# Top-k attention in four head pairs between the chunks of the output projection, with its weight pieces and both top-k searches in another order

## The chip, the cores and the metric

The kernel runs on one core of a Trainium2 chip. The metric is the device time in microseconds (us) of one execution; lower is better. The engines are TensorE (PE, matmuls; PEld, its weight loads), VectorE (DVE), ScalarE (ACT), GpSimd (POOL) and SyncE (SP, which here only issues weight transfers).

## What is computed

Four layers on 256 tokens of width 1024, in float32. The change touches one of them, the "even" layer: sparse attention and a pooling branch, whose results go through one output projection.

```python
def even_mixer(h, w_in, w_out, q_g, k_g, pool_w, pool_scale):
    q, k, v, qi, ki, wi, u = jnp.split(h @ w_in, offsets, axis=-1)
    q, k = rms_norm(q (8 heads of 64), q_g), rms_norm(k (2 heads of 64), k_g)
    attn = dsa_attention(q, k, v, qi, ki, wi)
    pooled = multiscale_pool(u, pool_w, pool_scale)     # 4 groups of 128 channels
    return concatenate([attn, pooled]) @ w_out          # 1024 x 1024

def dsa_attention(...):      # per block of 128 queries
    score = sum over 4 index heads of relu(qi . ki) * wi, causal
    sel = top_k(score, 64)                              # 64 keys of each query
    logits = q . k[sel] / 8;  p = softmax(logits);  o = p @ v[sel]
```

The kernel doesn't gather: it turns the top 64 of each query into an additive mask (0 or a very large negative number) and runs a dense softmax over all keys.

## The kernel before, in words

All weights stream through three raw buffers in SBUF (`raw_weights`), in the order that `weight_pieces()` writes out by hand; SP issues the transfer of piece n once the last use of piece n-3 is done. Each piece is cut into "halves". For every half ACT writes the rounded part (`w_hi`, line 1271) and DVE the rest (`w_lo`, line 1592) into one of four places, so half s can be written once TensorE has read half s-4. A product with a half is then three fp32r matmuls: hi*hi, hi*lo and lo*hi. The DVE and ACT programs call `advance(upto)` at fixed points, which writes all halves up to that number; a call placed behind other work waits for it, and TensorE with it.

`features` (lines 646, 647, 650) makes 128 output features of 256 tokens from a half. `out_half` (709, 710, 714) adds one chunk of 128 input channels to the output y, in 12 matmuls of 512 columns; `out_last_two` (733 to 735) does the last two chunks bank by bank, so that the four banks of y come one after the other. `add_y` (1648) adds y to x, `norm` (773, 1313, 1618) makes the normalized input of the next layer, and the feed-forward layer begins with `fresh_features` (629).

In the even layer before the change the halves are, counted from the layer's first: h0 to h3 index queries and small columns, h4 to h6 k and v (h6 is v, lines 1070 to 1072), h7 to h10 q, h11 to h14 u, then the pool's weights and h15 to h22 for the eight chunks of the output projection. TensorE, in order: projections of the index part; first half of k; the index products (1057); rest of k and v; q and u, with the sums of squares for the norms (`head_square_sums`, 907) between them; then `softmax_heads` over eight heads, one at a time: logits (1089), transposes of the probabilities (943), values (1099 to 1101); then the pool products (1116); then the eight chunks of the output projection, attention's four first.

DVE forms the score (1930 to 1936) and calls `choose` twice: eight rounds of `max` (1944) and `match_replace` (1946), with two calls of `advance` inside, and then ten small operations that form the mask (1949 to 1959). The first call, for the 256 keys of the second query block, stands behind the score. Then the three `normed` (1822) of k and q, and only then the second call, for the first block. ACT's part is the squares (1417), the inverse roots (`scale_unit`, 1424 and 1425), the exponentials (1458) and the copies of the transposed probabilities (1467). POOL makes the pool's running sums as soon as u is there (547 to 552), and splits the attention's outputs into hi and lo (`split_output`, 508 and 511). A projected block goes through the `units` 0 to 3 of PSUM in turn; unit n waits until unit n-4 has been read.

Of the kernel before, what the change touches and what calls it, by code (L numbers as in the profile page):

```python
# [49 lines left out]
def weight_pieces():  # L50
# [36 lines left out]
def units():  # L87
    out = []

    def add(stage, engines):  # L90
        out.extend((stage, e) for e in engines)

    add("norm0", "vvvv")
    add("a_f", "a" * 8)
    add("a_i", "a" * 8)
    add("a_q", "v" * 8)
    add("a_g", "a" * 8)
    add("norm1", "aaaa")
# [6 lines left out]
    add("ev_i", "aa")  # L105
    add("ev_k", "v")
    add("ev_v", "a")
    add("ev_q", "vv")
    add("ev_u", "aa")
    add("ev_pool", "vv")  # L110
# [12 lines left out]


def build(nc, a, const, mask, out):
# [7 lines left out]
    with ExitStack() as ctx:  # L133
# [83 lines left out]
        def y_bank(j, t, n):  # L217

            return ps[:, (0 if j in (1, 4) else 4) + 2 * t + n, :]
# [126 lines left out]
        for name in ("sig_ready ln_ready scan_ready exp_ready spread_ready spread_exp kin_ready "  # L346
# [6 lines left out]
                     "ev_mixed "  # L353
# [96 lines left out]
        OUT2 = 8  # L450

# [124 lines left out]
        def _(pe):  # L576
# [353 lines left out]
            def softmax_heads(pre, heads, logits, pv):  # L930

                for i in range(heads + 3):
                    if i < heads:
                        if i >= 2:
                            pe.wait_ge(st(pre + "_max"), i - 1)
                        logits(i, ps[:, 4 + i % 2, :]).then_inc(st(pre + "_logits"), 1)
                    if 2 <= i < heads + 2:
                        h = i - 2
                        pe.wait_ge(st(pre + "_prob"), h + 1)
                        if h >= 2:  # L940
                            pe.wait_ge(st(pre + "_tcopied"), h - 1)
                        for b in range(3):
                            ins = pe.transpose(ps[:, 6 + h % 2, b * P:(b + 1) * P], prob[:, h % 3, b * P:(b + 1) * P], ident)
                        ins.then_inc(st(pre + "_turned"), 1)
                    if i >= 3:
                        h = i - 3
                        pe.wait_ge(st(pre + "_tcopied"), h + 1)
                        pv(h)

# [100 lines left out]
            bank = open_unit("ev_k")  # L1050
            s = next_half("ev_kv")
            used(s, features(bank[:, 0:T], s, SELF))
            wait_read(pe, "ev_i", 1)
            for h in range(HIDX):
# [4 lines left out]
                ins.then_inc(st("ev_rel"), 1)  # L1059
            s = next_half("ev_kv")  # L1060
# [14 lines left out]
            pe.wait_ge(st("ev_relu"), HIDX)  # L1075
            head_square_sums(ones64, 16)
            project_features("ev_q", "ev_q", SELF)
            project_features("ev_q", "ev_q", SELF)
            head_square_sums(ones64, 17)
            project_features("ev_u", "ev_u", SELF)  # L1080
            head_square_sums(ones64, 18)
            project_features("ev_u", "ev_u", SELF)

            def ds_logits(h, bank):
                if h == 0:
                    wait_read(pe, "ev_q", 1)
                rows = slice(HD2 * (h % 2), HD2 * (h % 2) + HD2)
                for t in range(NT):
                    ins = pe.matmul(bank[:, P * t:P * t + P * (t + 1)], evq[rows, h // 2, t * P:(t + 1) * P],
                                    evk[rows, h // 4, 0:P * (t + 1)], start=True, stop=True)  # L1090
                return ins

            def ds_pv(h):
                if h % 2 == 0 and h >= 4:
                    pe.wait_ge(st("ds_out"), h // 2 - 1)
                rows = slice(HD2 * (h % 2), HD2 * (h % 2) + HD2)
                bank = ps[rows, (h // 2) % 2, :]
                vh = lambda s: evv[:, s, HD2 * (h // 4):HD2 * (h // 4) + HD2]
                pe.matmul(bank[:, 0:P], vh(0), probT[:, h % 2, 0:P], start=True, stop=True)
                pe.matmul(bank[:, P:T], vh(0), probT[:, h % 2, P:2 * P], start=True, stop=False)  # L1100
                pe.matmul(bank[:, P:T], vh(1), probT[:, h % 2, 2 * P:3 * P], start=False, stop=True)\
                    .then_inc(st("ds_o"), 1)

            pe.wait_ge(unit_free["a"], before("a", unit[0] - 1))
            pe.wait_ge(unit_free["v"], before("v", unit[0] - 1))
            softmax_heads("ds", HE, ds_logits, ds_pv)
            pe.wait_ge(st("ds_out"), HE // 2)
# [11 lines left out]
            out_project("ev_out", 8, OUT2, lambda k: pe.wait_ge(st("ds_split"), k + 1) if k < 4 else  # L1119
                        wait_read(pe, "ev_pool", (k - 4) // 2))  # L1120
# [134 lines left out]
        def _(act):  # L1255
# [146 lines left out]
            for u in range(4):  # L1402
# [6 lines left out]
                ("ev_k", 0), ("ev_q", 0), ("ev_q", 1)]  # L1409
# [40 lines left out]
            def softmax_heads(pre, heads):  # L1450
                for i in range(heads + 2):
                    if i < heads:
                        act.wait_ge(st(pre + "_max"), i + 1)
                        if i >= 3:
                            act.wait_ge(st(pre + "_turned"), i - 2)
                        for t, q in enumerate((Q0, Q1)):
                            c = 2 * (i % 2) + t
                            ins = act.activation(prob[:, i % 3, q], lg[:, i % 2, q], ACT.Exp,
                                                 bias=row_neg[:, c:c + 1], accum_out=row_sum[:, c:c + 1])
                            if t == 1:  # L1460
                                ins.then_inc(st(pre + "_exp"), 1)
                    if i >= 2:
                        h = i - 2
                        act.wait_ge(st(pre + "_turned"), h + 1)
                        if h >= 2:
                            act.wait_ge(st(pre + "_o"), h - 1)
                        act.activation(probT[:, h % 2, :], ps[:, 6 + h % 2, 0:S3], ACT.Copy)\
                            .then_inc(st(pre + "_tcopied"), 1)

# [39 lines left out]
            square_unit("ev_k", 0)  # L1509
            bank = unit_of("ev_v", 0)  # L1510
            act.activation(evv, bank[:, 0:T].rearrange("p (t d) -> p t d", t=2), ACT.Copy).then_inc(unit_free["a"], 1)
            scale_unit(16, HD2)
            square_unit("ev_q", 0)
            square_unit("ev_q", 1)
            scale_unit(17, HD2)
            for u in range(2):
# [3 lines left out]
                if u == 0:  # L1520
                    scale_unit(18, HD2)
            advance(unit_half[FIRST["ev_u"] + 1] + NSPLIT)
            softmax_heads("ds", HE)
# [50 lines left out]
        def _(dve):  # L1574
# [363 lines left out]
            def choose(q, n, ahead):  # L1938

                src = score[:, q]  # L1940
                for r in range(TOPK // 8):
                    if r % 4 == 2:
                        advance(ahead + r // 4)
# [4 lines left out]
                least = top8[:, 7:8]  # L1948
                dve.tensor_scalar(sel_eq[:, 0:n], score[:, q], least, None, ALU.is_equal)
# [11 lines left out]
            choose(Q1, T, e)  # L1961
            normed("ev_k", 0, 16, evk, ev_gain[:, 1:2])
            normed("ev_q", 0, 17, evq[:, 0:2, :], ev_q_gain)
            normed("ev_q", 1, 18, evq[:, 2:4, :], ev_q_gain)
            choose(Q0, P, unit_half[FIRST["ev_q"] + 1] + NSPLIT)

            def ds_out(h):
                if h % 2 == 1:
                    dve.wait_ge(st("ds_o"), h + 1)
                    if h >= 4:  # L1970
                        dve.wait_ge(st("ds_split"), h // 2 - 1)
                    dve.tensor_copy(o_full[:, (h // 2) % 2, :], ps[:, (h // 2) % 2, 0:T]).then_inc(st("ds_out"), 1)

            advance(unit_half[FIRST["ev_u"] + 1] + NSPLIT)
            softmax_heads("ds", HE, ev_bias_t, ds_out)
            for pair in range(2):
                bank = unit_of("ev_pool", pair)
                for j in range(2):
                    g = 2 * pair + j
                    link(dve.tensor_scalar(pooled[:, g, :], bank[:, j * T:(j + 1) * T],  # L1980
                                           col["ev_pool_scale_2"][:, g:g + 1], None, ALU.mult))
# [104 lines left out]
```

## Time and profile before

| | us |
|---|---|
| median of 3 runs | 1337.49 (1335.97 to 1373.87) |
| profiled execution, its own time | 1334.04 |
| its span, first to last instruction | 1332.3 |
| PE busy in the span | 1245.0 (93%) |
| DVE busy / ACT busy | 785.6 (59%) / 613.4 (46%) |
| mean granted clock of TensorE | 0.977 |

The span is what the trace's times refer to; 1.7 us lie around it. All places below are us from the span's start. The layer that the change touches lies between about 674 and 805. The granted clock is given as a share of full speed: 1.0 is 2.4 GHz, 0.5 is 1.2 GHz.

### The profile page before, as it was taken

To read this page: it belongs to the slowest core of one execution; us is meant where nothing else is said; L and a number is where in the kernel's file an instruction comes from. 1 tells how busy PE (TensorE), PEld (TensorE's weight loads), DVE (VectorE), ACT (ScalarE), POOL (GpSimd) and SP (SyncE) were. 2 spreads that over 40 slices of the span, in tenths; PEclk is the share of its full clock that TensorE was granted. 3 is DMA by queue.
4 is the path that set the end of the run, shared out by engine and by line. 5 is a ranking of instruction groups with operands and counts; after the bars stand their busy time and mean duration, and the time that the engine had idled before them with its cause. 6 is when DMAs were issued, how large, how long until landed. Compare 5 with 4: busy or idle time off the path is not lost.

```text
span 1332.3 us, 21042 instructions
## 1 busy us (share of the span) xinstructions
PE 1245.0 (93%) x8609; PEld 1139.1 (85%) x8609; DVE 785.6 (59%) x1245; ACT 613.4 (46%) x950; POOL 107.6 (8%) x172
## 2 busy tenths in 40 slices
PE   2899999998989899999998699999999999899998
PEld 2889989876789899887888479999989887899997
DVE  7888987654595354555546756555554433655554
ACT  2557623433455354554444335434453654544442
POOL 0200000031030000112100410000000133000000
PEclk9999999999999999999989589999999999999999
DMA  9896779402557465322522054555545322555552
GB/s 328 293 307 190 253 249 313 165 1 85 184 175 215 124 213 165 124 91 69 170 92 72 32 177 141 190 189 189 190 158 171 114 96 76 176 173 183 186 189 95
DMA packets 164880, 219.94 MB, mean 165 GB/s; under 512 B 5868, under 2 KB 135696, under 8 KB 164784
## 3 DMA queue, kind: packets, MB, share of 16 engines
q1 hardware_dynamic: 163984, 216.82, 50.3%
q0 software_dynamic: 800, 1.77, 0.4%
q8 instruction: 69, 1.13, 0.4%
q14 instruction: 27, 0.22, 0.0%
HBM read 217.53 MB, written 1.05 MB: 164 GB/s over the span
## 4 chain that ended last, share of the span: by engine, by line
PE 74%; DVE 12%; DMA 6%; ACT 6%; issue 2%; SPq 0%; ACTq 0%; DVEq 0%
PE ps L646 12%; PE ps L650 11%; PE ps L647 11%; PE ps L709 5%; PE ps L714 5%; PE ps L710 5%; DMA raw_weights<-in_a_w_in 4%; DVE w_lo L1592 4%; PE ps L687 3%; PE ps L682 3%; PE ps L683 3%; DVE acc L1674 2%; ACT w_hi L1271 1%; PE ps L962 1%; PE ps L907 1%
## 5 line engine op out<-in xcount | busy, mean ns | idle before, releaser
L1592 DVE TENSOR_TENSOR w_lo<-raw_weights,w_hi 128x1024 fp32r<-128x1024 f32 x348 | 423.7, 1228 | 282.3 <-ACT w_hi L1271 280.7
L1271 ACT ACTIVATE w_hi<-raw_weights 128x1024 fp32r<-128x1024 f32 x348 | 362.8, 1054 | 415.5 <-PE ps L714 110.6
L646 PE MATMUL ps<-act_hi,w_hi 128*128 128x256 f32 x1616 | 405.6, 289 | 3.8 <-ACT w_hi L1271 3.8
L647 PE MATMUL ps<-act_lo,w_hi 128*128 128x256 f32 x1616 | 397.4, 283 | 0.0
L646 PEld LDWEIGHTS ps<-act_hi,w_hi 128*128 128x128 f32 x1616 | 310.4, 192 | 12.1 <-issue 8.5
L647 PEld LDWEIGHTS ps<-act_lo,w_hi 128*128 128x128 f32 x1616 | 310.7, 192 | 3.3 <-issue 2.4
L650 PE MATMUL ps<-act_hi,w_lo 128*128 128x256 f32 x1616 | 228.0, 284 | 7.1 <-DVE w_lo L1592 7.1
L650 PEld LDWEIGHTS ps<-act_hi,w_lo 128*128 128x128 f32 x1616 | 209.2, 193 | 8.0 <-DVE w_lo L1592 7.9
L709 PE MATMUL ps<-w_hi,act_hi 128*128 128x512 f32 x320 | 126.7, 396 | 2.5 <-DVE work L1777 1.9
L710 PE MATMUL ps<-w_hi,act_lo 128*128 128x512 f32 x320 | 125.4, 392 | 0.0
L714 PE MATMUL ps<-w_lo,act_hi 128*128 128x512 f32 x320 | 86.9, 392 | 0.0
L1674 DVE SCALAR_TENSOR_TENSOR acc<-raw_weights,small,acc 128x512 f32<-128x512 f32 x112 | 84.1, 751 | 4.1 <-DMA raw_weights<-in_mod_w 0.5
L682 PE MATMUL ps<-w_hi,act_hi 128*128 128x256 f32 x320 | 81.0, 289 | 5.0 <-DVE big L1822 3.4
L683 PE MATMUL ps<-w_hi,act_lo 128*128 128x256 f32 x320 | 80.6, 288 | 0.0
L709 PEld LDWEIGHTS ps<-w_hi,act_hi 128*128 128x128 f32 x320 | 60.4, 189 | 16.1 <-DVE work L1777 2.3
L714 PEld LDWEIGHTS ps<-w_lo,act_hi 128*128 128x128 f32 x320 | 60.6, 190 | 12.8
L710 PEld LDWEIGHTS ps<-w_hi,act_lo 128*128 128x128 f32 x320 | 60.5, 189 | 11.8
L508 POOL CAST act_hi<-work 128x256 fp32r<-128x256 f32 x44 | 26.6, 604 | 519.2 <-DVE work L1782 255.9
L682 PEld LDWEIGHTS ps<-w_hi,act_hi 128*128 128x128 f32 x320 | 62.9, 197 | 6.1 <-DVE big L1822 4.2
L683 PEld LDWEIGHTS ps<-w_hi,act_lo 128*128 128x128 f32 x320 | 63.0, 197 | 0.2 <-issue 0.2
L1531 ACT ACTIVATE work<-ps 128x256 f32<-128x256 f32 x44 | 16.9, 385 | 68.3 <-PE ps L650 68.2
L687 PE MATMUL ps<-w_lo,act_hi 128*128 128x256 f32 x320 | 45.8, 287 | 0.3 <-DVE w_lo L1592 0.3
(258 smaller groups left out, 1421.4 us busy)
## 6 DMA issues: line engine op xcount, KB each, us to landing
raw_weights<-in_ffn_w SPq DMA_DIRECT2D x66, 1024.0 KB, 5.2
raw_weights<-in_a_w_in SPq DMA_DIRECT2D x32, 1024.0 KB, 6.1
raw_weights<-in_mod_w SPq DMA_DIRECT2D x24, 1024.0 KB, 5.9
raw_weights<-in_kv_w SPq DMA_DIRECT2D x16, 1024.0 KB, 5.6
raw_weights<-in_b_w_in SPq DMA_DIRECT2D x16, 1024.0 KB, 5.4
raw_weights<-in_od_w_qkv SPq DMA_DIRECT2D x12, 1024.0 KB, 5.2
raw_weights<-in_kv_mod_w SPq DMA_DIRECT2D x8, 1024.0 KB, 5.8
raw_weights<-in_a_w_out SPq DMA_DIRECT2D x8, 1024.0 KB, 5.0
```

Of the source, the lines that this page charges most:

```text
L646: pe.matmul(dst, wh[:, k, :], act_hi[:, base + k, :], start=(k == 0), stop=False)
L647: pe.matmul(dst, wh[:, k, :], act_lo[:, base + k, :], start=False, stop=False)
L650: ins = pe.matmul(dst, wl[:, k, :], act_hi[:, base + k, :], start=False, stop=(k == KD - 1))
L682: pe.matmul(dst, act_hi[:, base + k, tok], wh[:, k, :], start=(k == 0), stop=False)
L683: pe.matmul(dst, act_lo[:, base + k, tok], wh[:, k, :], start=False, stop=False)
L687: ins = pe.matmul(dst, act_hi[:, base + k, tok], wl[:, k, :], start=False, stop=(k == KD - 1))
L709: pe.matmul(dst, act_hi[:, chunk, tok], wh[:, cols_], start=first, stop=False)
L710: pe.matmul(dst, act_lo[:, chunk, tok], wh[:, cols_], start=False, stop=False)
L714: ins = pe.matmul(dst, act_hi[:, chunk, tok], wl[:, cols_], start=False, stop=last)
L1271: act.activation(half_view(w_hi, s), HALVES[s][2], ACT.Copy).then_inc(hi_done, 1)
L1592: dve.tensor_tensor(half_view(w_lo, s), HALVES[s][2], half_view(w_hi, s).bitcast(F32), ALU.subtract).then_inc(lo_done, 1)
L1674: ins = dve.scalar_tensor_tensor(out=acc[:, m % 2, :], in0=w[:, k, :], scalar=c, in1=acc[:, m % 2, :], op0=ALU.mult, op1=ALU.add)
```

## The change

1. Pieces: u, q, k, v instead of k, v, q, u, so h4 to h7 are u, h8 to h11 q, h12 and h13 k, h14 v. The output projection takes its pool chunks first: h15 to h18 are chunks 4 to 7, h19 to h22 chunks 0 to 3.
2. DVE: the first top-k call has five `advance` inside, the second follows directly behind it and the norm of the first half of q; the norms of q's second half and of k come last. The split of the pooled outputs is its own step.
3. ACT takes over the scaling of the pooled outputs from DVE, and the copy of the attention's outputs out of PSUM.
4. TensorE: the pool products go ahead of the attention. The eight heads become four pairs: logits, transposes and values of two heads are issued together, heads alternating, on two banks of banks 4 to 7. Between the steps stand the chunks of the output projection, whose y moves to banks 0 to 3. The last chunk alone is done bank by bank.
5. The buffers of the attention are sized for pairs, two deep.

```diff
-    pieces += [("ev_qi", 0), ("ev_small", 0), ("ev_kv", 0), ("ev_q", 0), ("ev_q", 1), ("ev_u", 0), ("ev_u", 1),
+    pieces += [("ev_qi", 0), ("ev_small", 0), ("ev_u", 0), ("ev_u", 1), ("ev_q", 0), ("ev_q", 1), ("ev_kv", 0),
                ("pool_w", 0)]
-    pieces += [("ev_out", n) for n in range(4)]
+    pieces += [("ev_out", n) for n in (2, 3, 0, 1)]
...
-            return ps[:, (0 if j in (1, 4) else 4) + 2 * t + n, :]
+            return ps[:, (0 if j in (1, 2, 4) else 4) + 2 * t + n, :]
...
+            def ds_logits(p):
+                if p == 0:
+                    wait_read(pe, "ev_k", 0)
+                if p == 2:
+                    wait_read(pe, "ev_q1", 0)
+                if p >= 2:
+                    pe.wait_ge(st("ds_out"), p - 1)
+                for t in range(NT):
+                    for e, rows in enumerate(pair_rows):
+                        ins = pe.matmul(ds_bank(p, e)[:, P * t:P * t + P * (t + 1)], evq[rows, p, t * P:(t + 1) * P],
+                                        evk[rows, p // 2, 0:P * (t + 1)], start=True, stop=True)
+                ins.then_inc(st("ds_logits"), 1)
+
+            def ds_turn(p):
+                pe.wait_ge(st("ds_prob"), p + 1)
...
+            def ds_pv(p):
+                pe.wait_ge(st("ds_tcopied"), p + 1)
+                if p == 0:
+                    wait_read(pe, "ev_v", 0)
+                v = [evv[:, s, HD2 * (p // 2):HD2 * (p // 2) + HD2] for s in range(NT)]
+                for e, rows in enumerate(pair_rows):
+                    pe.matmul(ds_bank(p, e)[rows, 0:T], v[0], ds_probT[:, e, 0:T], start=True, stop=False)
+                for e, rows in enumerate(pair_rows):
+                    ins = pe.matmul(ds_bank(p, e)[rows, P:T], v[1], ds_probT[:, e, T:S3], start=False, stop=True)
+                ins.then_inc(st("ds_o"), 1)
+
+            def ev_out_chunk(c):
+                if c == 4:
+                    pe.wait_ge(unit_free["a"], before("a", unit[0] - 1))
+                    pe.wait_ge(unit_free["v"], before("v", unit[0] - 1))
+                if c >= 4:
+                    pe.wait_ge(st("ev_pooled"), (c - 4) // 2 + 1)
+                else:
+                    pe.wait_ge(st("ds_split"), c + 1)
+                out_half("ev_out", OUT2 + c, c == 4, c == 3)
+
+            ds_logits(0)
+            ev_out_chunk(4)
+            ds_logits(1)
+            ev_out_chunk(5)
+            ds_turn(0)
+            ev_out_chunk(6)
+            ds_pv(0)
+            ds_turn(1)
+            ds_logits(2)
+            ev_out_chunk(7)
+            ds_pv(1)
+            ds_logits(3)
+            ev_out_chunk(0)
+            ds_turn(2)
+            ev_out_chunk(1)
+            ds_pv(2)
+            ds_turn(3)
+            ev_out_chunk(2)
+            ds_pv(3)
+            ev_out_chunk(3)
...
+            for pair in range(2):
+                bank = unit_of("ev_pool", pair)
+                for g in (2 * pair, 2 * pair + 1):
+                    ins = act.activation(pooled[:, g, :], bank[:, (g % 2) * T:(g % 2 + 1) * T], ACT.Copy,
+                                         scale=col["ev_pool_scale_2"][:, g:g + 1])
+                ins.then_inc(unit_free["a"], 1)
+            scale_unit(18, HD2)
...
+            first_out = first_half[AT[("ev_out", 2)]]
+            ds_exps(0)
+            advance(first_out + 3)
+            ds_exps(1)
+            advance(first_out + 4)
+            ds_take_turned(0)
+            advance(first_out + 5)
+            ds_take_out(0)
+            ds_take_turned(1)
+            advance(first_out + 6)
+            ds_exps(2)
+            ds_take_out(1)
+            advance(first_out + 7)
+            ds_exps(3)
+            ds_take_turned(2)
+            ds_take_out(2)
+            ds_take_turned(3)
+            ds_take_out(3)
...
+            last_i = unit_half[FIRST["ev_i"] + 1]
+            choose(Q1, T, {0: last_i + 4, 2: last_i + 5, 4: last_i + 6, 6: last_i + 7, 8: last_i + 8})
+            normed("ev_q0", 0, 16, evq[:, 0:2, :], ev_q_gain)
+            choose(Q0, P, {2: last_i + 9, 5: last_i + 10, 8: last_i + 11})
+            normed("ev_q1", 0, 17, evq[:, 2:4, :], ev_q_gain)
+            normed("ev_k", 0, 18, evk, ev_gain[:, 1:2])
+            first_out = first_half[AT[("ev_out", 2)]]
+            split_pooled(0)
+            ds_maxima(0)
+            advance(first_out + 3)
+            ds_scales(0)
+            split_pooled(1)
+            ds_maxima(1)
+            advance(first_out + 4)
+            ds_scales(1)
+            advance(first_out + 5)
+            ds_maxima(2)
+            advance(first_out + 6)
+            ds_scales(2)
+            ds_maxima(3)
+            advance(first_out + 7)
+            ds_scales(3)
```

`last_i` is h3, `first_out` is h15. `ds_exps` is four exponentials, `ds_take_turned` two copies of 128x384, `ds_take_out` two copies of 64x256, `ds_maxima` four masked maxima and one negation, `ds_scales` a reciprocal and four scalings.

## Rows read from the trace of the kernel before

**Rows 1.** Waits of PE, 660 to 800: total, times, longest.

```profile
PE ps L1089 <- ACT big L1518: 5.4, 1, 5.4
PE ps L1089 <- DVE small L1860: 5.2, 1, 5.2
PE ps L650 <- DVE w_lo L1592: 5.0, 2, 3.5
```

**Rows 2.** Chain that ended last, around attention: start, duration, what.

```profile
750.87 1.58 PE ps L1089 x4
752.44 0.83 PE ps L943 x3
...
754.75 1.58 PE ps L1089 x4
```

**Rows 3.** Busy time by window: PE, PEld, DVE, ACT, POOL; clock, DMA share, GB/s.

```profile
94.00:96.00 2.00, 2.00 (x11) 2.00 (x11) 1.71 (x2) 1.95 (x6) 0.00 (x0) 0.50 1.00 313
...
734.00:736.00 2.00, 1.22 (x8) 1.01 (x8) 1.83 (x10) 0.00 (x0) 1.74 (x3) 0.84 0.38 68
...
752.00:760.00 8.00, 8.00 (x28) 5.14 (x26) 2.85 (x16) 2.78 (x11) 0.00 (x0) 0.50 0.01 2
...
1100.00:1105.00 5.00, 5.00 (x26) 3.91 (x25) 1.69 (x2) 2.53 (x5) 2.59 (x4) 1.00 0.48 160
```

**Rows 4.** Chain that ended last, the other attention layer's projection.

```profile
1106.68 0.57 PE ps L1200 x2
...
1107.48 0.63 PE ps L1176 x2
...
1108.32 0.43 PE ps L709
...
1110.36 0.91 PE ps L714 x4
```

**Rows 5.** Timeline of PE: start, duration, line, tile; in brackets the idle time before.

```profile
698.85 0.22 PE L1070 MATMUL ps<-w_hi,act_hi 128*128 128x128 f32 x1
...
704.16 1.07 PE L907 MATMUL ps<-work,cst 128*128 128x512 f32 x2
...
740.82 1.66 PE L1089 MATMUL ps<-big 64*128 64x128 f32 x8 [5.38 <-ACT big L1518]
...
775.20 1.99 PE L1116 MATMUL ps<-big,raw_weights 128*128 128x256 f32 x8 [0.52 <-DVE work L1972]
```

**Rows 6.** Chain that ended last, the third pass of one half of `features`.

```profile
847.17 0.96 PE ps L650 x8
```

**Rows 7.** Timeline of DVE, the two top-k searches.

```profile
699.33 0.43 DVE L1944 MAX8 small<-big 128x8 f32<-128x256 f32 x1
...
712.42 0.75 DVE L1822 SCALAR_TENSOR_TENSOR big<-ps,cols,work 128x512 f32<-128x512 f32 x1
...
731.18 0.28 DVE L1944 MAX8 small<-big 128x8 f32<-128x128 f32 x1
...
742.36 4.07 DVE L1592 TENSOR_TENSOR w_lo<-raw_weights,w_hi 128x1024 fp32r<-128x1024 f32 x3
```

**Rows 8.** The page's costliest groups: busy, mean ns.

```profile
L1592 DVE TENSOR_TENSOR w_lo<-raw_weights,w_hi 128x1024 fp32r<-128x1024 f32 x348 | 423.7, 1228 | 282.3 <-ACT w_hi L1271 280.7
```

**Rows 9.** Timelines of ACT and POOL: one split, one copy, one output.

```profile
727.62 1.06 ACT L1271 ACTIVATE w_hi<-raw_weights 128x1024 fp32r<-128x1024 f32 x1 [5.97 <-DMA raw_weights<-in_ev_w_out]
...
751.59 0.47 ACT L1467 ACTIVATE work<-ps 128x384 f32<-128x384 f32 x1
...
762.62 0.72 POOL L511 TENSOR_TENSOR act_lo<-work,act_hi 128x256 fp32r<-128x256 f32 x1
```

**Rows 10.** Chain that ended last: exponentials, and the end of the projection.

```profile
747.64 0.99 ACT big L1458 x4
...
795.96 0.61 DVE x L1648
...
805.01 0.36 PE ps L629
```

More of the change, by code:

```diff
@@ L1074, in _ @@
             used(s)
[L1075 to L1107, printed above, removed]
             n = AT[("pool_w", 0)]
@@ L1519, in _ @@
                     .then_inc(unit_free["a"], 1)
[L1520 to L1523, printed above, removed]
+            square_unit("ev_q0", 0)
+            square_unit("ev_q1", 0)
+            scale_unit(16, HD2)
+            square_unit("ev_k", 0)
+            scale_unit(17, HD2)
+            bank = unit_of("ev_v", 0)
+            act.activation(evv, bank[:, 0:T].rearrange("p (t d) -> p t d", t=2), ACT.Copy).then_inc(unit_free["a"], 1)
@@ new lines, in _, with ds_exps @@
+            for pair in range(2):
[5 more added lines that the diff above has]
+            scale_unit(18, HD2)
+            def ds_exps(p):
+                act.wait_ge(st("ds_max"), p + 1)
+                if p >= 2:
+                    act.wait_ge(st("ds_turned"), p - 1)
+                for e in range(2):
+                    for t, q in enumerate((Q0, Q1)):
+                        c = 2 * e + t
+                        ins = act.activation(ds_prob[:, p % 2, e, q], ds_lg[:, e, q], ACT.Exp,
+                                             bias=ds_neg[:, p % 2, c:c + 1], accum_out=ds_sum[:, p % 2, c:c + 1])
+                ins.then_inc(st("ds_exp"), 1)
@@ L1936, in _, with choose @@
             link(dve.tensor_tensor(score, score, causal, ALU.add))
-            def choose(q, n, ahead):
+            def choose(q, n, splits):
                 src = score[:, q]
                 for r in range(TOPK // 8):
-                    if r % 4 == 2:
-                        advance(ahead + r // 4)
+                    if r in splits:
+                        advance(splits[r])
                     link(dve.max(top8, src))
@@ L1948, in choose @@
                 least = top8[:, 7:8]
+                if TOPK // 8 in splits:
+                    advance(splits[TOPK // 8])
                 dve.tensor_scalar(sel_eq[:, 0:n], score[:, q], least, None, ALU.is_equal)
@@ L1974, in _, with split_pooled @@
[L1974 to L1981, printed above, removed]
+            def split_pooled(pair):
+                wait_read(dve, "ev_pool", pair)
@@ new lines, in ds_maxima @@
+            def ds_maxima(p):
+                dve.wait_ge(st("ds_logits"), p + 1)
+                for e in range(2):
+                    for t, q in enumerate((Q0, Q1)):
+                        c = 2 * e + t
+                        ins = dve.tensor_tensor_reduce(out=ds_lg[:, e, q], in0=ds_bank(p, e)[:, q], in1=ev_bias_t[:, q],
+                                                       scale=1.0, scalar=LOW, op0=ALU.add, op1=ALU.max,
+                                                       accum_out=ds_max_[:, p % 2, c:c + 1])
+                link(ins)
+                dve.tensor_scalar(ds_neg[:, p % 2, :], ds_max_[:, p % 2, :], -1.0, None, ALU.mult)\
+                    .then_inc(st("ds_max"), 1)
```

124 lines of the change are left out of this document (58 added, 66 removed).

## The prediction

> **What bounds the kernel now.** I read the page first (PE busy 93% of the span), then PE's waits between 660 and 800, then the chain that ended last in that stretch, then its busy time by window. After 805 PE runs without a gap into the feed-forward layer, so every microsecond by which this layer ends earlier is one off the span. Three waits of PE stand out: 5.4 before the first logits, 5.2 before the third, 5.0 in two halves of `features` [rows 1]. All three are DVE's doing: the second top-k call (731.18) starts only behind the three norms, and the last w_lo are written only behind it, to 746.4 [rows 7]. The third thing is the attention itself. One head takes 1.58 for logits, 0.83 for transposes and, to the next logits at 754.75, 1.48 for values [rows 2]. The windows show why: PE counts as busy all of 752 to 760, at a granted clock of 0.50 (1.2 GHz), after it fell in 734 to 736 behind the idle stretches [rows 3]. The other attention layer, which puts a dense chunk between its small matmuls, keeps 1.00 in 1100 to 1105 [rows 3]; there logits take 0.84 (1107.48 to 1108.32) and values 0.80 (1106.68 to 1107.48) [rows 4].
>
> **The stretch to be compared** begins at 698.85 on PE [rows 5], up to which both kernels do work of the same shapes (u's first half in place of k's), and ends with the first addition to x at 795.96; from there to the next layer's first matmul it is 9.05 in both [rows 10], as the same `norm` follows. Before, it is 97.1: eight halves of `features` 23.0 (8 x 24 matmuls, 8 in 0.96 [rows 6]), v 5.3 (698.85 to 704.16), three sums of squares 2.7, pool 2.0 [rows 5]; projection to the first x 18.9 (from 777.0 on); attention 28.0 (1.66 for the first two logits, 1.58, and 749.97 to 774.70 [rows 2, 5]); waits some 17 (the 15.6 of [rows 1] and small ones).
>
> **Part by part.**
>
> *Attention on PE.* Four pairs. Logits of two heads lie on different rows of the array: the first two heads before took 1.66 together, and a single head 1.58 [rows 2, 5]. So a pair costs one head, 0.84 at full clock. Six transposes: 2 x 0.83 at half clock, 0.86 at full. Values of a pair, alternating over column halves: no row shows such a pair; between 0.80 (as if side by side) and 1.6 (two heads in series) [rows 4]; I take 1.1, since the logits are the nearest relative and did overlap, but here the operands are full height. Sum 4 x 2.8 = 11.2 instead of 28.0: 16.8 less, of which 8 to 9 is the clock. The Trainium skill ("TensorEngine Tiling (Array Packing)", Key Properties) says that different tiles run in parallel, but that a change of tiling mode drains the engine. By its first half alone values would be 0.80 and the sum 1.2 less. Its second half speaks against interleaving, and the trace has a price for it: next.
>
> *Chunks between the pieces.* A chunk is 12 matmuls, 4 in 0.91, so 2.72, and the first behind small matmuls takes 0.43 instead of 0.23 [rows 4]: 2.92. Seven of them cost 1.4 more. y's banks 0 to 3 are also those of `norm`; `norm` waits for x bank by bank already, and the 9.05 hold there. The last chunk alone is bank by bank: 0.9 from its start to the first y.
>
> *The halves' order, and DVE.* A step of DVE: w_lo 1.17 to 1.23 [rows 8]. The first top-k call takes 13.1 (699.33 to 712.42) with two w_lo in it [rows 7], so 10.8 bare; with five inside, 16.6: 715.9. PE meanwhile does h6 to h11, 698.85 + 6 x 2.88 = 716.1, and each w_lo comes before its third pass: no wait in place of the 1.5 there. Then the sum of squares of q (0.9), ACT's two steps (1.4), the norm at 718.5 to 719.2. The second call (11.2 from 731.18 with two w_lo and mask; bare 8.1) holds h13 after 5 rounds (3.6) and h14 after 8: w_lo at 724.0 and 726.9. PE has done h12 and the sum and is at h13's third pass at 722.7, so it waits **1.3**, then **1.9** before v (`wait_lo` stands ahead of v). v, pool and the third sum end at 735.1.
>
> *DMA and SP.* The piece behind pool_w waits for h14's w_lo, 726.9, and lands some 5 later, 732.5. ACT's `advance` for h17 stands ahead of the copies of v and of the pool, and ahead of the roots for k. So ACT: h17 to 733.6, v 0.4, pool 1.5 (to 735.6), roots to 736.9; DVE: norm of k to 737.7; first logits at 737.8, a wait of **2.6**. This is now the late thing: before it was 740.82, but with the pool still to do.
>
> *The interleaved part*, walked in the order of the three programs, with four exponentials 2.0, two copies 0.95, the two copies out 0.75, w_hi 1.06 [rows 9, 10], maxima 1.75, scalings 1.3, POOL's split 1.3 (0.72 is its second half [rows 9]). Waits of PE: 0.3 for the pool's split (added ahead of the maxima on DVE); 0.7 before the transposes of pair 0 (exponentials to 742.7, then w_hi of h18 on ACT, then its w_lo on DVE, then the scalings to 746.2); 0.3; **2.9** before the values of pair 0 (exponentials of pair 1 to 751.2, w_hi of h19, then the copy of pair 0's transposes to 753.2: ACT's order, not data); 0.5; 0.8 for pair 1's output, for which logits of pair 3 wait; 1.3 and **2.2** at the end, where values, ACT's copy, POOL's split and the chunk come one behind the other. Together 14.9 with the three above. Queued behind each waiting ACT or DVE step are only later splits, whose places are free by then. Last chunk at 778.5; first y at 779.4; DVE has h24's w_lo until 780.4, because ACT makes h23 and h24 behind its last copy; first x at 780.5.
>
> *Sum:* 23.0 + 5.3 + 2.7 + 2.0 + 7 x 2.92 + 0.9 + 11.2 + 14.9 + 1.1 = 81.5 against 97.1: 15.6 less.
>
> *The clock.* In the new order PE is idle 1.9 at 725, 2.6 at 735 and 2.9 at 750. In the stretch before 734 to 736, 3.5 of waiting for a w_lo was followed by a fall; elsewhere a short dip covers 94 to 96 with PE busy [rows 3]. A dip among dense matmuls lasts about 3.3 in this trace (94 to 97), and costs half: 1.6. I expect one on PE's path: 1.6 off the gain; bounds none, and three (4.9). **Gain 14.0.** The Trainium skill ("TensorE: Matmul & The Clock Gate", What's actually happening) says the clock is low by default and sustained activity releases it. The row of 752 to 760 doesn't fit a reading of that by busy time, as PE was busy throughout and stayed at 0.50; it fits one by how densely the array is fed.
>
> Profiled execution: 1334.04 - 14.0 = 1320.0 (span 1318.3). The runs' median is 3.45 above the profiled time; from it, 1337.49 - 14.0 = 1323.5.
>
> **Rivals.**
>
> A, *ACT and DVE in series become the bound.* Each pair passes DVE, ACT, DVE, PE, ACT, PE, and `advance` stands between. If values run in series (1.6), logits too (1.68), I walk to a first x 3.8 later; with three dips in place of one another 3.3; a transfer that lands in 8 instead of 5 adds 2 to 3 at 732. Gain 4 to 10, in the middle 7: 1330.5. For it: three of my large waits lie on that chain. Against it: ACT was idle for more than half of it before.
>
> B, *deeper cover.* Values side by side, no dip, the waits of 2.9 and 2.2 smaller by half: gain 17 to 21, 1318.5. Against it: the two waits come from the written order of ACT.
>
> C, *slower: the clock stays at 0.50 through the interleaved part.* Then a chunk is 5.6, logits 1.6, transposes 1.7, values 2.2, and the same walk ends 24 later than mine: first x at 804.4, 8.4 behind the kernel before: 1346. It decides at seven chunks: with each of them at half clock the loss of 2.7 a chunk (19) exceeds the gain. For it: before, 22 us of busy PE didn't bring the clock back. Against it: the other attention layer at 1.00 with the same mix of one chunk and 2.7 of small matmuls [rows 3, 4].
>
> D, *it doesn't do what it says*: PE's order is overlapped on paper, but waits just move, so that what the attention gives (16.8) is taken by new waits over 30 instead of 14.9: 1337.
>
> **How the numbers follow.** Forecast (gain 11 to 17) 0.56; A 0.24; B 0.12; C 0.05; D 0.03. The range takes A down to a gain of 6 and B up to one of 20: 1317.5 to 1331.5, and leaves out C, D and A's end. 2% of 1337 is 27, about what a measurement of this kernel can tell from no change. A gain of 27 would need PE's waits under 4 with all else as walked: 0.03. C at its full price is 8 behind, so slower by over 2% needs a longer half clock than the layer is: 0.01. Within 2%: 0.96.
>
> **What would show it.** In the new trace: no wait of PE between 699 and 716; two short ones at h13 and v; first logits near 738; clock 1.00 in most windows of 738 to 780; logits of a pair in about 0.84, values in 0.8 to 1.6; the largest wait in the interleaved part before the values of pair 0, released by ACT's copy; first x near 780 to 782 and the next layer's first matmul near 790. It would be wrong if the clock sits at 0.50 beyond one dip, if waits of PE from 698 to 780 sum to over 20, or if time moves in the layers that nothing here touches.

## The result, and the profile after

| | before | after |
|---|---|---|
| median | 1336.2 (15 runs) | 1327.22 (15 runs) |
| profiled execution, its own time | 1334.04 | 1329.57 |
| its span | 1332.3 | 1327.8 |
| mean granted clock | 0.977 | 0.978 |

The ratio is 0.9916, with an interval of 0.9892 to 0.994: 11.2 us less, between 8 and 14. A few executions of either kernel are disturbed and some 30 to 45 us longer; the medians of the table count them in (9.0 apart), all ratios leave them out, and no reading below uses a profile of one. Forecast was 14.0 less, 1323.5.

The two spans differ by only 4.5, because TensorE's clock fell for longer in layers that the change doesn't touch: the first matmul of this layer already comes 5.2 later after, and behind the layer the two are alike. So I measure the layer by itself, from its first `fresh_features` matmul to the same matmul of the next layer. Before it takes 674.18 to 805.01, 130.8; after 679.37 to 800.56, 121.2. That is 9.6 less in the layer, and 5.1 more outside of it. The following table divides it, with four of the experiments:

| us | fresh start to h5's third pass | to first logits | to first x | to next layer | layer |
|---|---|---|---|---|---|
| before | 23.7 | 42.9 | 55.1 | 9.05 | 130.8 |
| after | 25.4 | 46.6 | 40.2 | 9.05 | 121.2 |
| e9: attention first, then chunks | 23.8 | 46.6 | 49.7 | 9.15 | 129.2 |
| e1: early halves | 25.4 | 37.4 | 39.9 | 10.4 | 113.2 |
| e5: the same, second search last | 22.2 | 36.3 | 47.8 | 10.25 | 116.6 |
| e8: e1 and the tail | 23.8 | 37.4 | 38.8 | 9.1 | 109.1 |

Before has the pool's products (2.0) in its third column, all others in the second.

The first column is a warning. Up to h5's third pass all these kernels run matmuls of the same number, order and shapes, and yet it is 22.2 to 25.4 long. All of the difference is one fall of the clock near 690, behind or among the four-column products of h3. It lasted 3.3 in e5, 6.8 before and in e8 and e9 (and in b1 and e4, below), and 10 after and in e1, always over that same sequence, with PE busy:

```profile
690.00:692.00 2.00, 2.00 (x11) 2.00 (x11) 0.00 (x0) 0.00 (x0) 0.00 (x0) 0.50 0.03 6
692.00:694.00 2.00, 2.00 (x19) 1.85 (x18) 0.00 (x0) 0.00 (x0) 0.00 (x0) 0.92 0.00 0
```

```profile
692.00:694.00 2.00, 2.00 (x11) 2.00 (x11) 0.00 (x0) 0.00 (x0) 0.00 (x0) 0.50 0.00 0
```

(e5 first, then e1; columns as in [rows 3].) So the layer of one profile carries up to 3.2 that no edit made, and I compare kernels from h5's third pass to the first x where it matters: 98.1 before, 86.7 after, 77.3 in e1.

The waits of PE between 660 and 810, after (total, times, longest), to be held against [rows 1]:

```profile
PE ps L719 <- POOL act_lo L521: 3.5, 2, 2.1
PE ps L1101 <- DVE big L1882: 2.3, 1, 2.3
...
PE ps L1072 <- DVE w_lo L1652: 1.8, 1, 1.8
PE ps L660 <- DVE w_lo L1652: 1.4, 1, 1.4
PE ps L1119 <- ACT work L1557: 1.1, 1, 1.1
PE ps L1101 <- ACT work L1564: 0.9, 1, 0.9
PE ps L1110 <- DVE big L2050: 0.8, 1, 0.8
```

The three large waits of before, of 5.4, 5.2 and 5.0, are gone. What is left, beside those of the `norm` at either end of the layer, are seven kinds, each with a place in the walk: 1.4 at h13 (L660), 1.8 before v (L1072), 2.3 before the first logits (L1101), then small ones and the two for POOL's split ahead of the last two chunks (L719).

The chain that ended last, after, answers to [rows 2, 10]:

```profile
734.27 0.30 PE ps L1072
...
744.20 3.52 PE ps L1085 x8
747.72 1.34 PE ps L917 x2
...
751.34 1.14 PE ps L1101 x8
...
766.81 0.88 PE ps L1110 x6
767.68 0.86 PE ps L1101 x8
...
771.49 0.58 PE ps L1119 x4
772.07 0.24 PE ps L1121 x4
...
791.51 0.61 DVE x L1708
```

Read two things. A pair costs 0.86 for its logits (L1101), 0.88 for its six transposes (L1110) and 0.58 + 0.24 = 0.82 for its values (L1119, L1121): 2.56 for two heads, where one head took 3.9 before [rows 2]. But v takes from 734.27 to 744.20, 9.9, where it took 5.3 [rows 5], and the pool's products 3.5 where they took 2.0. The windows say why (columns: PE, PEld, DVE, ACT, POOL busy, then the granted clock):

```profile
730.00:732.00 2.00, 0.72 (x6) 0.72 (x7) 1.93 (x5) 0.00 (x0) 0.00 (x0) 1.00 0.00 0
732.00:734.00 2.00, 0.49 (x5) 0.28 (x3) 1.90 (x5) 1.45 (x3) 0.00 (x0) 1.00 0.01 4
734.00:736.00 2.00, 1.73 (x11) 1.76 (x12) 1.83 (x9) 0.36 (x1) 0.00 (x0) 0.72 0.41 49
736.00:738.00 2.00, 2.00 (x11) 2.00 (x11) 1.93 (x4) 0.00 (x0) 0.00 (x0) 0.50 0.95 381
...
748.00:750.00 2.00, 1.04 (x2) 0.00 (x0) 0.00 (x0) 1.48 (x4) 0.00 (x0) 0.87 0.54 111
...
752.00:754.00 2.00, 1.83 (x7) 1.16 (x4) 1.81 (x11) 0.07 (x1) 0.00 (x0) 0.50 1.04 426
754.00:756.00 2.00, 2.00 (x7) 1.57 (x6) 1.02 (x1) 2.00 (x9) 0.00 (x0) 0.66 0.24 98
...
770.00:772.00 2.00, 2.00 (x13) 1.34 (x13) 1.19 (x2) 1.87 (x8) 0.00 (x0) 1.00 1.08 382
```

Around the two waits for w_lo PE is busy only 0.72 and 0.49 of 2.00. Then the clock falls to 0.50 (1.2 GHz) and stays there for some 14 us, with PE busy all the time. It is back at 1.00 when PE waits 2.3 for the first logits, and behind that wait it falls again, from 752 to 755: the first logits take 1.14 instead of 0.86, and they and the first chunk 5.5 instead of 3.8. From 756 to 788 the interleaved part runs at 1.00; a third fall, 789.5 to 792.5, lies over the last chunk and costs nothing that shows: the first x waits for DVE's last w_lo there (789.13 to 791.51 in the chain), and behind it the layer takes 9.05 as before.

### The profile page after: what moved, and what is told of

The parts are those of the page before. It is cut to its first block, busy times and chain, and to the rows that moved or that the text cites. A ratio compares the mean times of both kernels' runs of the same rounds, so it can differ in the third digit from the quotient of the medians.

```text
span 1327.8 us, 20990 instructions
## 1 busy us (share of the span) xinstructions
PE 1243.0 (94%) x8593; PEld 1139.3 (86%) x8593; DVE 780.6 (59%) x1229; ACT 618.2 (47%) x962; POOL 110.0 (8%) x172
## 4 chain that ended last, share of the span: by engine, by line
PE 76%; DVE 11%; ACT 5%; DMA 5%; issue 2%; SPq 0%; POOL 0%; ACTq 0%; DVEq 0%
PE ps L656 12%; PE ps L660 12%; PE ps L657 12%; PE ps L719 5%; PE ps L720 5%; PE ps L724 5%; DVE w_lo L1652 3%; DMA raw_weights<-in_a_w_in 3%; PE ps L697 3%; PE ps L692 3%; PE ps L693 3%; DVE acc L1734 1%; ACT w_hi L1304 1%; PE ps L917 1%; PE ps L952 1%
## 5 line engine op out<-in xcount | busy, mean ns | idle before, releaser
L660 PE MATMUL ps<-act_hi,w_lo 128*128 128x256 f32 x1616 | 228.2, 284 | 1.9 <-DVE w_lo L1652 1.9
L660 PEld LDWEIGHTS ps<-act_hi,w_lo 128*128 128x128 f32 x1616 | 209.7, 193 | 2.5 <-DVE w_lo L1652 2.5
L719 PE MATMUL ps<-w_hi,act_hi 128*128 128x512 f32 x328 | 132.6, 404 | 5.8 <-POOL act_lo L521 4.1
L720 PE MATMUL ps<-w_hi,act_lo 128*128 128x512 f32 x328 | 130.5, 398 | 0.0
L719 PEld LDWEIGHTS ps<-w_hi,act_hi 128*128 128x128 f32 x328 | 63.0, 192 | 22.3 <-POOL act_lo L521 5.0
```

What stands on the lines that cost most here:

```text
L660: ins = pe.matmul(dst, wl[:, k, :], act_hi[:, base + k, :], start=False, stop=(k == KD - 1))
L719: pe.matmul(dst, act_hi[:, chunk, tok], wh[:, cols_], start=first, stop=False)
L720: pe.matmul(dst, act_lo[:, chunk, tok], wh[:, cols_], start=False, stop=False)
```

## The experiments

My theory after the first look: the interleaving works as walked, and what the forecast lacks is the half clock over v, set off by the waits for w_lo at h13 and v. Rival readings: the waits themselves are the whole price and the clock is chance; the order of the halves alone brings the gain; the interleaving brings it by the values' alternation only.

**e1, the two early halves.** DVE makes the w_lo of h12 to h14 before the second search, which is left undivided.

```diff
+            advance(last_i + 11)
             normed("ev_q0", 0, 16, evq[:, 0:2, :], ev_q_gain)
-            choose(Q0, P, {2: last_i + 9, 5: last_i + 10, 8: last_i + 11})
+            choose(Q0, P, {})
```

> The changed kernel, with the w_lo of k's two halves and of v written directly behind the first top-k search, not inside the second. Theory: the two short waits of PE at h13 and v (1.4 and 1.8) made the clock fall, and as v's 128-column products and the pool follow, it didn't come back for 14 us. Then both waits go, v takes 5.3 instead of 9.9, the pool 2.0 instead of 3.5, and the layer (121.2 from its first matmul to that of the next) comes to 111 to 112; against the kernel before some 20 us, ratio 0.983 to 0.986. Rival: v, pool and sum of squares are thin enough to pull the clock down by themselves; then only the waits' 3.2 go, v stays near 10 and the layer near 118, ratio 0.989.

Measured: 1317.03 (5 runs), ratio 0.9865 (0.9842 to 0.9889); the layer 113.2, 8.0 less than after and 1 to 2 above what I expected. Its waits, same stretch:

```profile
PE ps L1101 <- DVE big L1882: 2.3, 1, 2.3
PE ps L1119 <- ACT work L1557: 1.9, 1, 1.9
...
PE ps L1085 <- DVE big L1882: 0.9, 1, 0.9
```

and two of its windows:

```profile
734.00:736.00 2.00, 0.09 (x1) 0.00 (x0) 0.73 (x2) 1.42 (x3) 0.00 (x0) 1.00 0.70 197
...
744.00:746.00 2.00, 2.00 (x13) 1.53 (x12) 1.97 (x9) 0.00 (x0) 0.00 (x0) 1.00 0.89 259
```

The waits at h13 and v are gone (3.2), and with them the fall of the clock: v takes 5.3 again (724.85 to 730.16), 4.6 less. Ahead of the first logits 9.1 is saved: 3.2 and 6.6, less a new wait of 0.9 before the pool's products (L1085), for a PSUM bank that DVE's `normed` frees; at the other end 1.3 was lost again in the norm, where the clock fell at 780. Removing 3.2 of waiting gave 8.0: the clock was the larger part. The seven profiles of kernels in the new order agree: v took 9.6 to 9.9 in the three whose w_lo of h12 to h14 lie inside the second search (after, e4, e9), and 5.3 in the four where they come early (e1, e2, e5, e8).

The window of 734 to 736 also shows that one idle stretch of 2.3 before the first logits can leave the clock at 1.00. It did in e1, e2 and e8; behind the same 2.3 the clock fell in after, e4, e5 and e9. So whether a single wait of this length costs a fall can't be told from these traces. That e1 lacks the fall at 752 gained it only 0.3 on the way to the first x (39.9 against 40.2): the wait before the values of pair 0, for ACT's copy, grew from 1.1 to 1.9 instead.

**e3 and e9, the attention first.** All of the change but the interleaving: four pairs one behind the other, then eight chunks.

```diff
+            for c in (4, 5, 6, 7, 0, 1, 2, 3):
+                ev_out_chunk(c)
...
             ds_logits(0)
-            ev_out_chunk(4)
             ds_logits(1)
-            ev_out_chunk(5)
             ds_turn(0)
-            ev_out_chunk(6)
             ds_pv(0)
```

(the `+` lines stand behind the last `ds_pv`; of the `advance` calls of ACT and DVE between the pairs three are left, for h17 and h18)

> The changed kernel, with PE's pairs first and all eight chunks behind them; the searches and the piece order stay. Theory: the dense chunks between the pieces are what keeps the clock at 1.00 and cover the way through DVE and ACT. Then the granted clock is 0.50 for most of the attention, its pieces take twice as long, PE waits over 10 in it, and the layer is 12 to 20 longer than 121.2. Rival: pairing and the early pool are what helps; then the attention costs its 11 us of matmuls plus the waits that the chunks hid badly anyway, and the layer stays within 4 of 121.2.

Measured: 1336.57 (10 runs), ratio 1.0003 (0.9985 to 1.002), 11.6 slower than after. For a profile the same kernel ran again:

> The same kernel as e3_attention_first, for a profile. If the 11.6 that the chunks between the pairs are worth lie in waits of PE, its waits between the first logits and the first chunk sum to 8 or more, and its layer is 131 to 134 long against 121.2; if they lie in the clock, the windows between the first logits and the first chunk show 0.50 throughout and the waits sum to under 4. I expect both: waits of 8, and 3 to 4 from the clock.

Measured: 1335.68 (one run), the layer 129.2, 2 under what I expected; from h5's third pass to the first x it is 96.3, 9.6 more than after. In its chain:

```profile
757.26 1.12 PE ps L1119 x4
758.38 0.43 PE ps L1121 x4
758.81 1.47 PE ps L1110 x6
...
765.51 1.68 PE ps L1101 x8
...
776.31 0.43 PE ps L719
```

In its waits, and in its windows:

```profile
PE ps L1119 <- ACT work L1551: 7.3, 3, 3.5
PE ps L1110 <- DVE big L2040: 3.4, 1, 3.4
PE ps L1101 <- ACT work L1558: 3.3, 1, 3.3
```

```profile
748.00:752.00 4.00, 0.88 (x6) 0.16 (x2) 2.00 (x12) 1.86 (x8) 0.00 (x0) 0.50 0.41 170
...
768.00:772.00 4.00, 1.17 (x7) 0.58 (x8) 2.89 (x11) 2.73 (x10) 0.00 (x0) 0.50 0.23 47
```

From the first logits (746.55) to the first chunk (776.31) 29.8 pass for four pairs that need 4 x 2.56 = 10.2 at full clock. 14.0 are waits, more than I expected; most of the rest is the half clock (1.47, 1.68 and 1.12 + 0.43 in place of 0.88, 0.86 and 0.82), which lies over most of the attention; only around 762 and behind 775 is it 1.00. Interleaved, the part from the first logits to the first x takes 40.2 instead of 49.7. So the gain of the change hangs on the chunks that stand between: 9.6 of the 11.3 by the traces, all of it by the times of e3. They fill the waits, and with PE thus filled the clock is at 1.00 from 756 on. The new order, the pairs and the early pool without them gain nothing that the times of e3 show.

**b1, the searches alone.** The kernel before, with the second search directly behind the first and five more `advance` in the two.

```diff
-            choose(Q1, T, e)
+            choose(Q1, T, {2: e, 6: e + 1})
+            choose(Q0, P, {0: e + 2, 3: e + 3, 6: e + 4})
             normed("ev_k", 0, 16, evk, ev_gain[:, 1:2])
...
-            choose(Q0, P, unit_half[FIRST["ev_q"] + 1] + NSPLIT)
```

> The kernel before, with the second top-k search directly behind the first and nothing else moved (its w_lo at rounds 0, 3 and 6). Theory: the waits of 5.4 and 5.2 before the logits go, but heads stay one by one without chunks, so the clock falls during them all the same: the attention still takes 24 to 25 and the gain is 8 to 10 us, ratio 0.993. Rival: the clock fell before only because of those waits, and without them stays up; then the attention takes 16 and the gain is 16 to 18, more than the whole change gave.

Measured: 1334.75 (12 runs), ratio 0.9986 (0.9957 to 1.0016), the layer 130.8 as before. The expectation failed. Its waits:

```profile
PE ps L646 <- DVE big L1822: 5.5, 1, 5.5
PE ps L1089 <- ACT big L1518: 5.3, 1, 5.3
PE ps L1089 <- DVE small L1860: 1.9, 1, 1.9
PE ps L650 <- DVE w_lo L1592: 1.0, 2, 0.8
```

The waits for w_lo fell from 5.0 to 1.0 and that for the third logits from 5.2 to 1.9, but that for the first logits stayed (5.3 against 5.4), and a new one of 5.5 came: PE can't open the next unit of `features` until DVE's `normed` (L1822) has read a PSUM bank, and the norms now stand behind both searches. The chain goes on through the transfers that this delays:

```profile
724.69 0.74 DVE big L1822
725.44 1.14 DVE w_lo L1592
726.60 5.93 DMA raw_weights<-in_ev_w_out
...
736.19 1.67 DVE w_lo L1592
737.87 4.91 DMA raw_weights<-in_ev_w_out
```

So the search's place alone pays nothing. In the new order the first halves that PE makes beside the searches are u's, whose banks ACT reads, and there DVE's late norms hold nobody up: after has no such wait. That the new order alone would do is not shown; no run has it with the search at its old place between the norms.

**e5, the second search last.** e1, but with `choose(Q0, P, {})` behind `normed("ev_k", ...)`, and the `advance` for the three early halves behind the norm of q's first half instead of ahead of it.

> The changed kernel, with the w_lo of k and v early and the second top-k search back behind the norm of k. Theory: the search (8 us with its mask) then lies between k's norm and the first maxima, on PE's way, with only one chunk and one pair of logits as cover (3.8); PE waits 4 or more near the first transposes and the clock dips; the layer is 6 to 9 longer than in the kernel with the early w_lo, that is 118 to 120. Rival: PE has chunks 4 and 5 and a pair of logits to do and loses less than 2.

Measured: 1324.62 (4 runs), ratio 0.9916 (0.9889 to 0.9943), the layer 116.6, 3.4 more than e1 where 6 to 9 were expected. But the fall near 690 was shorter here, which took 3.2 off the first column of the table and has nothing to do with the edit. From h5's third pass to the first x e5 takes 84.1, e1 77.3: 6.7 more, and the ratios say the same (0.9916 against 0.9865, 6.8). So the theory held. The first logits come 1.1 earlier, mostly because the wait of 0.9 before the pool's products is gone. Then one wait costs more than that:

```profile
PE ps L719 <- DVE act_lo L2029: 7.5, 1, 7.5
```

The first chunk needs the split of the pooled outputs, which DVE has queued behind the search, and the clock is at 0.50 from 734 to 747. From the first logits to the first x it is 7.8 longer than in e1.

**e2, small matmuls mixed among dense ones.** The fall near 690, among or behind the small four-column products of h3, comes in all these kernels. e2 is e1 with the 48 of them strewn, two by two, among the 24 matmuls of h4; h5 also moves ahead of the index products.

```diff
-                    pe.matmul(dst, act_hi[:, k, tok], wh[:, k, :], start=(k == 0), stop=False)
+                    small.append((dst, act_hi[:, k, tok], wh[:, k, :], k == 0, False))
...
+            for n, (l, r, first, last) in enumerate(big_mms):
+                for dst, sl, sr, sfirst, slast in small[2 * n:2 * n + 2]:
+                    ins_small = pe.matmul(dst, sl, sr, start=sfirst, stop=slast, skip_group_check=True)
```

> As the kernel with the early w_lo, and the 48 four-column products of the index weights are issued between the 24 products of h4, two before each. In both kernels the clock falls while the 48 stand alone (5.4 us) and stays at 0.50 through h4. Theory: what counts is how densely the array is fed, so mixed with 256-column products they don't pull the clock down: no fall near 690, the layer 2.5 to 3.5 shorter. Rival: any stretch with this many small products does it, mixed or not: the fall comes later, over h4 and h5, and the layer gains nothing or loses 2.

Measured: 1320.67 (4 runs), ratio 0.9897 (0.9877 to 0.9917), the layer 115.9, 2.7 more than e1's.

```profile
686.00:688.00 2.00, 2.00 (x20) 2.00 (x19) 0.00 (x0) 0.00 (x0) 0.00 (x0) 1.00 0.97 311
688.00:690.00 2.00, 2.00 (x13) 2.00 (x12) 0.00 (x0) 0.00 (x0) 0.00 (x0) 0.55 0.56 192
690.00:694.00 4.00, 4.00 (x20) 4.00 (x21) 0.00 (x0) 0.00 (x0) 0.00 (x0) 0.50 0.01 3
```

The clock falls at 688 with PE busy throughout, and stays down until 698, 10 us as in e1; a new wait of 1.9 for a w_lo comes with the edit. Mixing didn't prevent the fall, as the rival said. The theory's forecast failed; that how densely the array is fed decides, which the prediction remarks too, is neither borne out nor ruled out by it.

**e4, the heads of a pair in series.** `for e, rows` outside of `for t` in the logits, and each head's two value products together.

> The changed kernel, with logits and values of a pair issued head after head instead of alternating. Theory: only alternation puts two heads side by side on the array; then values of a pair take 1.6 instead of 0.82 and logits 1.6 instead of 0.85. Rival: the order doesn't matter for logits (the kernel before had two heads in a row in the time of one), and values stay at 0.82 too.

Measured: 1327.14 (one run), the layer 119.5. Its values of a pair:

```profile
761.65 0.66 PE L1119 MATMUL ps<-work,big 128*64 128x256 f32 x4 [0.89 <-ACT work L1556]
762.13 0.40 PE L1120 MATMUL ps<-work,big 128*64 128x128 f32 x4
```

Start to end this is 0.88 (0.87 after, read in the same way), and logits show 0.93 in both kernels; from h5's third pass to the first x it is 86.6 against 86.7. The order in which the two heads are issued makes no difference; that only alternation overlaps them is false. The shorter layer is the fall near 690 again.

**e7 and e8, the tail.** DVE's last w_lo before the additions to x wait for ACT, which makes h23 and h24 behind its last copy. In e7 (on e2) and e8 (on e1) the two halves stand ahead of that copy.

```diff
             ds_take_turned(3)
+            advance(first_half[AT[("w1", 0, 0)]] + 1)
             ds_take_out(3)
-            advance(first_half[AT[("w1", 0, 0)]] + 1)
```

> As the kernel with the small products among h4's, and ACT writes the first two w_hi of the next layer ahead of the last copy out of the attention, so that their w_lo on DVE don't stand before the first addition to x. Theory: the first x comes 1.0 to 1.3 earlier, the layer is 1 shorter than that one's. Rival: the clock dip at the last chunk or the copies themselves come last, and nothing changes.

Measured: 1318.79 (6 runs), ratio 0.9876 (0.9855 to 0.9897) against e2's 0.9897: less by 2.8, but the intervals overlap, so nothing can be told.

> The kernel with the two early halves and the undivided second search, and in it only ACT's last copy moved behind the halves for h23 and h24. If the last copy and the two halves (0.53 each) stand on the path to the last chunk, nothing is to be had: PE would wait 1.1 longer for the last copy of the attention's output and 1.3 less at the norm behind it, so 0 to 1 less, ratio 0.985 to 0.987, the layer 112.5 to 113.5. The rival, that the order at the end costs nothing at all because DVE's additions to x set it, gives the same layer of 113.2 within 0.3.

Measured: 1315.36 (6 runs), ratio 0.9853 (0.982 to 0.9886), the layer 109.1, shorter than either theory gave (112.5 to 113.5). From the first logits to the first x it is 38.8 against 39.9 in e1, 1.1 less; the norm behind it is 1.3 shorter, as the clock didn't fall there (e1: 0.57 in 780 to 784, e8: 1.00); and 1.6 lie in the fall near 690, where the two kernels are the same. Its ratio is no further from e1's than that. It is the fastest kernel measured, 20 below before, and can't be told from e1.

## Why the prediction was near, and where it was off

The time came out 3.7 above the forecast, inside the range. The measured gain of 11.2 is at the lower end of the forecast's case (11 to 17). That it is so near is in part luck: the clock cost 8.3 where 1.6 was put, and the interleaved part, that cost left out, was 4.2 shorter than walked; so 4.2 of the 6.7 that were missing hid in the other error. Two of the prediction's own signs of being wrong came true: the clock sat at 0.50 beyond one dip, and time moved in layers that nothing touches. The third didn't: PE's waits between 698 and 780, as walked, sum to 12, not over 20. The profiled execution, forecast at 1320.0, took 1329.57. Of these 9.6, 5.1 lie outside of the layer, 1.7 in the longer fall near 690, and 2.7 in the stretch that the prediction walked. And the runs tell apart much smaller differences than the 2% that the prediction names: the ratio's interval is a quarter of a percent to either side. To compare with the walk I take 6.88 off the times of after, so that the end of h11 falls on the walked 716.13.

- *Up to h14, as walked.* PE has no wait up to h13, then 1.4 (walked 1.3), with h13's w_lo at 724.3 (724.0), and 1.8 before v (1.9).
- *The first search, 1.8 too short.* It ends at 717.7, not 715.9. I took bare durations from a stretch in which POOL is idle; here POOL runs at the same time. No cost came of it on PE. No run takes POOL's work away, so that POOL is the cause is likely and not shown.
- *The step that failed: the clock's term.* "A dip among dense matmuls lasts about 3.3 in this trace (94 to 97), and costs half: 1.6. I expect one on PE's path." There were two on it. The first came where it was expected, behind the 1.8 at v, but it lasted 14 and cost 4.6 in v and 2.0 in the pool's products and the sum of squares: 6.6, beyond my bound of 4.9 for three. The second, behind the wait for the first logits, lasted 3.3 and cost 1.7. So 8.3 instead of 1.6. The size came from a single fall, and the same trace had longer ones: 6.8 near 690, with 0.95 in 684 to 688, 0.50 in 688 to 692 and 0.70 in 692 to 696, and 22 us of busy PE in the attention. The shape of the matmuls doesn't tell them apart. The fall of 94 to 97 ran over matmuls of 256 columns,

```profile
94.13 0.41 PE L682 MATMUL ps<-w_hi,act_hi 128*128 128x256 f32 x1
```

and near 690 one and the same sequence of matmuls was slow for 3.3, 6.8 or 10 from kernel to kernel. Over v it was 14 in all three profiles that have a fall there (after, e4, e9). e1 shows the term: without the two waits the fall is gone and v is back at 5.3.

- *The pair, 0.3 too dear.* Values took 0.82, walked at 1.1 between 0.80 and 1.6; logits 0.86 (0.84), transposes 0.88 (0.86). The Trainium skill ("TensorEngine Tiling (Array Packing)", Key Properties) says that different tiles run in parallel; with 0.82 for a pair, as much as one head of the other layer [rows 4], the trace agrees, for column halves as for row halves.
- *The interleaved part, 4.2 too long.* 40.2 against 42.7 walked, and 1.7 of the 40.2 are the second fall, which the walk holds apart. The four pairs give 1.0 of the 4.2. Waits of PE in it sum to 6.5, not 9.0; the largest walked one, 2.9 before the values of pair 0, is 1.1. The two at the end, 1.3 and 2.2, are 1.3 and 2.1.
- *The sum.* 15.6 - 8.3 + 4.2 = 11.5; measured from h5's third pass to the first x it is 98.1 before (697.89 to 795.96) and 86.7 after (704.77 to 791.51), 11.3 less. The layer as a whole shows 9.6, because the fall near 690, ahead of that stretch, lasted some 10 us after and 7 before; e1, e5 and e8, the same up to there, differ by up to 3.2 in the same place, so I take this for chance.
- *Rival C* was right in kind and wrong in place: the clock did stay at 0.50 long, but over v, not over the interleaved part. e9 shows where C's mechanism lives: without the chunks most of the attention is at 0.50 again.
- *"For it: three of my large waits lie on that chain"* (A): they were as large as walked or smaller, and didn't grow. But A's price for three dips, 3.3 more than for one, was nearer to the clock's cost than the forecast's.

What stays open is why the fall near 690 comes in every kernel and why it lasts 3.3 in one and 10 in another, and whether the waits or the half clock would dominate in e9 if one of them were taken away alone; neither was tried.

## What to carry to other kernels

Before pricing a fall of the clock, list every one in the trace, and give its term the whole spread of their lengths rather than the shortest; here 3.3 to 10 over the same matmuls, and 14 over v, where two waits of 1.4 and 1.8 cost 3.2 and pulled 6.6 behind them. When two kernels are compared by one profile each, compare a stretch that leaves out such a fall where both run the same work: e5's cost read as 3.4 with it and is 6.7 without. When an engine's long serial work (a search, a scan) is moved ahead, move it only together with the buffers that its successors on that engine must release: alone its move gave nothing that can be measured (b1), and in the new order the place of three short steps around it was worth 8 to 9 (e1). Small dependent matmuls were cheap here when dense, independent ones stood between them, twice over: the waits were filled, and the clock stayed up (756 to 788 after, against mostly 0.50 in e9).

## What the runs showed of the hardware

- With the clock at 0.50, PE and its weight loads busy 2.00 of 2.00, v's 128-column matmuls ran for up to 10 us without getting it back (9.9 after, 9.7 in e9 from 729.48 to 739.14; 5.3 at 1.00). The Trainium skill ("TensorE: Matmul & The Clock Gate", What's actually happening) says that the default is the throttled state and that activity releases it. By PE's busy time the trace doesn't agree; here the clock rose only in the window of 748 to 750, in which the last sum of squares, of 512-column matmuls, ends.
- The clock can fall from 1.00 to 0.50 with no idle time of PE ahead of it: near 690 in every kernel, in e2 among mixed four- and 256-column matmuls (PE busy 2.00 of 2.00 in 686 to 690). And a fall over the same matmuls can last 3.3, 6.8 or 10 (e5, before, e1).
- Some of DVE's steps took longer beside a busy POOL. The same scan over 128 x 256 took 0.69 before, with POOL idle, and 1.09 after, with POOL busy; one w_lo took 1.59 instead of 1.23. The three w_lo behind it in the same search (1.22 to 1.23) and its `max` and `match_replace` (0.42 and 0.41) took no longer beside it. First before, then after:

```profile
709.92 0.69 DVE L1953 TENSOR_TENSOR_SCAN big<-big 128x256 f32<-128x256 f32 x1
```

```profile
721.08 1.09 DVE L2015 TENSOR_TENSOR_SCAN big<-big 128x256 f32<-128x256 f32 x1
```
